# Sixty-four-column products of a recurrence, each given as two products of half the output partitions

## The chip, the cores and the metric

The kernel runs on one core of a Trainium2 chip. TensorE multiplies a stationary operand (up to 128 rows of contraction by 128 columns, which become output partitions) with moving columns and writes to PSUM. VectorE (DVE in the profile), ScalarE (ACT) and GpSimd (POOL) work on what it leaves, and SyncE (SP) issues most DMAs. The metric is the device time of one execution in microseconds (us), lower is better. Before the change it is 2248.54 us, the median of three runs (2246.16 to 2250.44).

## The reference, cut to what matters

Two encoder layers over 256 tokens of width 1024: dilated attention and a dense SwiGLU, then bidirectional RWKV-7 time mixing and eight SwiGLU experts of which each token takes two. All is float32. The change is in the RWKV-7 recurrence, which the reference writes as a scan over tokens with one 64 x 64 state per head:

```python
def step(state, inp):
    r_t, w_t, k_t, v_t, a_t, b_t = inp
    sa = jnp.einsum('bhvk,bhk->bhv', state, a_t)
    state = state * w_t[:, :, None, :] + sa[..., None] * b_t[:, :, None, :] + v_t[..., None] * k_t[:, :, None, :]
    return state, jnp.einsum('bhvk,bhk->bhv', state, r_t)
...
y_f = wkv_scan(rf, decay[0], k_dir[0], vf, -kk, kk * a[0], reverse=False)
y_b = wkv_scan(rf, decay[1], k_dir[1], vf, -kk, kk * a[1], reverse=True)
```

There are 16 heads of 64 features and two directions.

## The kernel before, in words

The kernel has no scan over tokens. Time is cut in two chunks of 128 tokens (t = 0, 1), and inside a chunk the recurrence is a triangular system of 128 x 128 for each head and direction. Heads are handled in four quarters (q = 0 to 3) of four heads. A set is one of the four pairs of direction and chunk.

For each quarter TensorE makes, in the order of its one queue:

- `decay_sums`, `cumulated`, `ends`: sums over time from which ScalarE takes exponentials, and from these VectorE the scaled keys (L1814 to L1835);
- `operands` (transposes, L920 and L921) and `system`: products over 64 rows, two heads side by side on the lower and the upper 64 rows of the array;
- `pairings`: again 64 rows, two heads side by side, evicted by VectorE with a mask (L1863, L1865, L1866);
- `values`: for each of four heads a product of a 128 x 128 stationary matrix with the 64 columns of that head's values (`z0`, PSUM bank 7), evicted by ScalarE (L1455), and a second such product that `add_y` (L957) accumulates in bank 4;
- `head_turn`: the solve. The early chunk of both directions goes first (steps z1 to z5, width 64), the late chunk after it with the width 128. The helper `four` gives the four products of a step, and VectorE (L1897, L1904) or ScalarE (L1474) evicts them before the next step of the same direction may start (`need`). The two directions alternate, so that one's products cover the other's eviction. Products that were already 64 output partitions wide are z5 and the chunk states (`St`).

The turns are software pipelined. `head_turn(q)` also gives the decay sums, operands and systems of quarter q + 1, and it ends with `all_pairings(q + 1)`; VectorE meanwhile computes that quarter's keys among the z evictions, and in the late half the inverse of 16 x 16 diagonal blocks by many small linked instructions (L1876, L1878), which go out and come back by DMA (`td`, `gt_in`). A turn takes some 68 us, and all four with the first pairings run from 726.6 to 986 us.

`run` (L682) gives one chain of accumulating products to one output; `mm` is the plain matmul. A float32 product leaves two MATMUL records and two LDWEIGHTS records in the trace, called two passes below; a transpose leaves one. In the shapes of the profile, `128*128 128x64` is a pass with 128 contraction rows, 128 stationary columns and 64 moving columns, and `128*64` one with 64 stationary columns, `64*128` one with 64 contraction rows.

Of the kernel before, what the change touches and what calls it, by code (L numbers as in the profile page):

```python
# [22 lines left out]
P = 128  # L23
# [16 lines left out]
RH = 64  # L40
RQ = 256
# [101 lines left out]
def build(nc, x_in, pos_in, const_in, mask_in, vec_in, rows_in, qk_rows, qk_cols, wqkv, awo, wrkv, w0, w1, w2, a0, a1, a2,  # L143
          g1, g2, bwo, fw13, fw2, router, mw13, mw2, out):
    ctx = ExitStack()
    with ctx:
        arena = ctx.enter_context(nc.sbuf_tensor("arena", [P, 53200], F32))
        ps = ctx.enter_context(nc.psum_tensor("ps", [P, 8, 512], F32))
# [152 lines left out]
        for d in range(2):  # L301
            o = {}
# [20 lines left out]
        gm23 = [[lent.take(4, P) for _ in range(2)] for _ in range(2)]  # L323
# [58 lines left out]
        def at_set(q, i):  # L382

            return q * 4 + i + 1
# [291 lines left out]
        def _(pe):  # L676
            mm = pe.matmul

            def run(o, pairs, **kw):

                for n, (a, b) in enumerate(pairs):
                    last = mm(o, a, b, start=(n == 0), stop=(n == len(pairs) - 1))  # L682
                return last

            def rms_transposes(n, src, t, bank0):

                pe.wait_ge(rms_xn, n * T + t + 1)
                for b in range(4):
                    for f in range(2):
                        c = (2 * b + f) * P  # L690
                        last = pe.transpose(ps[:, bank0 + b, f * S + t * P:f * S + (t + 1) * P], src[:, t, c:c + P], ident)  # L691
                    last.then_inc(rms_tp, 1)
# [74 lines left out]

            pe.wait_ge(in_const, 16)
            rms_transposes(0, attn, 0, 0)
            rms_transposes(0, attn, 1, 0)  # L770
            for hg in range(HG):
                def qk_transposes(j):
# [11 lines left out]
                for j in range(18):  # L784
                    u = hg * 9 + j // 2
                    c = hg * 18 + j
                    t = j % 2
# [5 lines left out]
                    for k in range(KB):  # L793
                        if c == 0:
                            pe.wait_ge(rms_h, k + 1)
                        last = mm(ps[:, 4 + c % 2, :], hT[:, k, t * P:(t + 1) * P], w[:, k, :], start=(k == 0), stop=(k == KB - 1))  # L796
# [20 lines left out]
                for j in range(8):  # L817
                    h, t, c = j // 2, j % 2, hg * 8 + j
# [3 lines left out]
                    for b in range(4):  # L822
                        last = pe.transpose(ps[:, 6, b * P:(b + 1) * P], probs[:, c % 3, b * P:(b + 1) * P], ident)
# [4 lines left out]
                    if c >= 2:  # L828
# [3 lines left out]
                                           (pT[:, c % 2, 2], v[:, t, 1, hc]), (pT[:, c % 2, 3], v[:, t, 2, hc])]).then_inc(o_ps, 1)  # L832
            back_transposes(attn, 0, oT_ps, (o_sb, 16))
            out_projection(0, U_QKV, oT, (oT_sb, 4), lambda: rms_transposes(1, attn, 0, 4))

            rms_transposes(1, attn, 1, 4)
# [6 lines left out]
            for half in range(2):  # L843
                for n in range(2):
                    w = unit(RKV0 + n).rearrange("p (k n) -> p k n", n=512)
                    for t in range(T):
                        for k in range(4 * half, 4 * half + 4):
                            if (n, t) == (0, 0):
                                pe.wait_ge(mix_ready, k + 1)
                            last = mm(ps[:, 4 + 2 * n + t, :], MIXES[0][2][:, k, t * P:(t + 1) * P], w[:, k, :], start=(k == 0), stop=(k == KB - 1))  # L850
# [24 lines left out]
            def value(q, t, h):  # L875
                return rkv[:, 2, t, q * RQ + h * RH:q * RQ + (h + 1) * RH]
# [76 lines left out]

            def add_y(t, h, lhsT, rhs, first=False, last=False):

                c = t * RQ + h * RH
                return mm(ps[:, 4, c:c + RH], lhsT, rhs, start=first, stop=last, skip_group_check=True)  # L957

            def values(q, i):

                d, t = SETS[i]
                if i == 0 and q:
                    pe.wait_ge(Y.sb, q)
                pe.wait_ge(gm.sb, q * 8 + 2 * i + 2)
                if i:
                    pe.wait_ge(z0.sb, at_set(q, i - 1))
                for h in range(4):
                    c = h * RH
                    last = run(ps[:, 7, c:c + RH], [(gm23[i % 2][0][:, h, :], value(q, t, h))])
                last.then_inc(z0.ps, 1)  # L970
                for h in range(4):
                    add_y(t, h, gm23[i % 2][1][:, h, :], value(q, t, h), first=(i == 0 and h == 0))

            def all_pairings(q):

                pe.wait_ge(X.sb, 4 * (q + 1))
                pairings(q, 0)
                pairings(q, 1)
                values(q, 0)
                pairings(q, 2)  # L980
                values(q, 1)
                pairings(q, 3)
                values(q, 2)
                values(q, 3)

            def chain_of(q, late):


                turn = [16 * late]

                def four(done, of, by, width=P, rows=slice(0, P)):

                    bank = 5 + turn[0] % 3
                    turn[0] += 1
                    for h in range(4):
                        last = run(ps[rows, bank, h * width:(h + 1) * width], [(of[:, h, rows], by[:, h, :])])
                    last.then_inc(done.ps, 1)

                return four, turn
# [5 lines left out]
            def head_turn(q):  # L1005
# [51 lines left out]
                def early_y():  # L1057

                    for d in range(2):
                        need(z5, 0, d)  # L1060
                        for h in range(4):
                            add_y(d, h, gm1[2 * d][:, h, :], ze[d][0][:, h, :])
# [70 lines left out]
                for d in range(2):  # L1133
                    for h in range(4):
                        add_y(1 - d, h, gm1[2 * d + 1][:, h, :], zl[d][0][:, h, 0:RH])
# [56 lines left out]
            for t in range(T):  # L1192
                for n in range(2):
                    if (t, n) == (1, 1):
                        rms_transposes(3, xn, 0, 0)
                    for k in range(4, KB):
                        last = mm(ps[:, 4 + 2 * n + t, :], moT[:, k, t * P:(t + 1) * P], w[n][:, k, :], start=False, stop=(k == KB - 1))  # L1197
# [5 lines left out]
            for t in range(T):  # L1203
                last = run(ps[:, 4, t * EXPERTS:(t + 1) * EXPERTS], [(hT[:, k, t * P:(t + 1) * P], rw[:, k, :]) for k in range(KB)])
# [89 lines left out]
            with pe.Fori(0, EXPERTS // 2 - 1) as i:  # L1294
                for e in range(2):
                    n = i * 2 + e
                    one_expert(n, e, i, (lambda: row_transposes(n + 2, 0), lambda: row_transposes(n + 2, 1)))
            n = EXPERTS - 2
# [6 lines left out]
            with pe.Fori(0, OVER) as j:  # L1305
                with pe.If(j < many):
# [3 lines left out]
                    n = j + EXPERTS  # L1310
# [1069 lines left out]
```

## Time and profile before

| | |
|---|---|
| median of the three runs | 2248.54 us |
| the profiled execution's own time | 2250.66 us |
| its span, first to last instruction | 2248.8 us |
| mean granted TensorE clock | 0.988 |
| TensorE busy | 2178.3 us, 97% |
| VectorE busy | 429.4 us, 19% |
| chain that ended last | PE 92%, DVE 4%, ACT 2%, DMA 1%, issue 1% |

A PE record begins when the pass begins, and its end is modelled, so that passes overlap in the records; the distance between starts is the pace. A row of a group gives the count of records, the time in which at least one of them ran, the mean length of one in ns and the idle time before them with what ended it. Idle times under 0.15 us are not named.

### The profile page before, as it was taken

To read this page: it belongs to the slowest core of one execution; us is meant where nothing else is said; L and a number is where in the kernel's file an instruction comes from. 1 tells how busy PE (TensorE), PEld (TensorE's weight loads), DVE (VectorE), ACT (ScalarE), POOL (GpSimd) and SP (SyncE) were. 2 spreads that over 40 slices of the span, in tenths; PEclk is the share of its full clock that TensorE was granted. 3 is DMA by queue.
4 is the path that set the end of the run, shared out by engine and by line. 5 is a ranking of instruction groups with operands and counts; after the bars stand their busy time and mean duration, and the time that the engine had idled before them with its cause. 6 is when DMAs were issued, how large, how long until landed. Compare 5 with 4: busy or idle time off the path is not lost.

```text
span 2248.8 us, 19811 instructions
## 1 busy us (share of the span) xinstructions
PE 2178.3 (97%) x7756; PEld 1209.4 (54%) x7756; DVE 429.4 (19%) x960; ACT 296.0 (13%) x661; POOL 196.8 (9%) x318
## 2 busy tenths in 40 slices
PE   8999989999899999997999999999999999999998
PEld 3454456776455999875444444444444444444443
DVE  2131231000445467434000000000000000000100
ACT  2121130000012543310000000000000000000000
POOL 1111101000104354200000000000000000000000
PEclk9999999999999999997999999999999999999999
DMA  9433425445410110236988989889898898999991
GB/s 346 150 113 112 150 75 187 150 150 164 150 33 9 19 26 16 79 101 222 323 300 302 308 287 322 300 301 308 299 308 300 296 314 298 307 308 299 340 301 60
DMA packets 353293, 474.12 MB, mean 211 GB/s; under 512 B 30104, under 2 KB 288432, under 8 KB 353216
## 3 DMA queue, kind: packets, MB, share of 16 engines
q1 hardware_dynamic: 349856, 460.96, 61.3%
q0 software_dynamic: 2336, 8.42, 1.1%
q10 hardware_dynamic: 1024, 3.67, 0.4%
q8 instruction: 52, 0.85, 0.2%
q14 instruction: 25, 0.20, 0.0%
HBM read 460.96 MB, written 12.06 MB: 210 GB/s over the span
## 4 chain that ended last, share of the span: by engine, by line
PE 92%; DVE 4%; ACT 2%; DMA 1%; issue 1%; POOL 0%; SPq 0%; DVEq 0%; POOLq 0%
PE ps L682 47%; PE ps L1283 17%; PE ps L796 11%; PE ps L734 7%; PE ps L747 2%; PE ps L957 1%; PE ps L850 1%; PE ps L1258 1%; PE ps L763 1%; PE ps L1190 1%; PE ps L1197 0%; PE ps L781 0%; DMA arena<-yd,arena 0%; ACT arena L1439 0%; PE ps L691 0%
## 5 line engine op out<-in xcount | busy, mean ns | idle before, releaser
L682 PE MATMUL ps<-arena 128*128 128x512 f32 (+10 forms) x4290 | 1160.9, 435 | 28.4 <-ACT arena L1381 6.8
L682 PEld LDWEIGHTS ps<-arena 128*128 128x128 f32 (+3 forms) x4290 | 628.0, 188 | 509.8 <-issue 460.7
L1283 PE MATMUL ps<-arena 128*128 128x512 f32 x896 | 394.4, 593 | 1.5 <-ACT arena L1567 0.6
L1283 PEld LDWEIGHTS ps<-arena 128*128 128x128 f32 x896 | 165.8, 190 | 190.7 <-issue 190.7
L796 PE MATMUL ps<-arena 128*128 128x512 f32 x576 | 253.3, 596 | 2.6 <-DVE arena L1633 2.6
L2093 DVE TENSOR_TENSOR arena<-arena,ps 128x256 f32<-128x256 f32 x112 | 47.2, 421 | 999.7 <-ACT arena L1574 998.7
L796 PEld LDWEIGHTS ps<-arena 128*128 128x128 f32 x576 | 108.0, 191 | 129.3 <-issue 126.0
L1574 ACT ACTIVATE arena<-ps 128x256 f32<-128x256 f32 x112 | 43.1, 385 | 999.3 <-PE ps L682 999.3
L734 PE MATMUL ps<-arena 128*128 128x256 f32 x704 | 153.9, 381 | 0.0
L734 PEld LDWEIGHTS ps<-arena 128*128 128x128 f32 x704 | 134.6, 191 | 20.2 <-issue 1.9
L2343 POOL DMA_INDIRECT arena<-yd,arena x4 | 3.8, 957 | 1040.7 <-DMA yd<-arena 1039.8
L1258 PEld LDWEIGHTS ps<-arena 128*128 128x128 f32 x224 | 31.3, 141 | 55.3 <-issue 54.3
L747 PE MATMUL ps<-arena 128*128 128x512 f32 x128 | 55.6, 592 | 0.0
L1474 ACT ACTIVATE arena<-ps 128x512 f32<-128x512 f32 (+1 forms) x80 | 44.2, 559 | 54.7 <-PE ps L682 54.7
L1567 ACT ACTIVATE arena<-ps 128x256 f32<-128x256 f32 x112 | 42.4, 379 | 49.8 <-PE ps L1258 49.8
L1672 DVE TENSOR_TENSOR arena<-arena,ps 128x256 f32<-128x256 f32 x22 | 9.3, 422 | 198.6 <-ACT arena L1338 198.6
L1258 PE MATMUL ps<-arena 128*128 128x128 f32 x224 | 42.8, 273 | 0.2 <-DVE arena L2093 0.2
L1718 DVE TENSOR_REDUCE arena<-arena 128x4 f32<-128x512 f32 x24 | 16.5, 686 | 131.0 <-ACT arena L1363 131.0
L957 PE MATMUL ps<-arena 128*128 128x64 f32 x320 | 40.3, 277 | 0.0
L747 PEld LDWEIGHTS ps<-arena 128*128 128x128 f32 x128 | 24.3, 190 | 28.9 <-issue 28.7
L957 PEld LDWEIGHTS ps<-arena 128*128 128x128 f32 x320 | 37.8, 192 | 1.3 <-issue 0.7
L2257 POOL TENSOR_TENSOR arena<-arena 128x256 f32<-128x256 f32 (+4 forms) x70 | 34.7, 496 | 5.5
(238 smaller groups left out, 968.7 us busy)
## 6 DMA issues: line engine op xcount, KB each, us to landing
arena<-mw SPq DMA_DIRECT2D x336, 1024.0 KB, 6.9
arena<-wqkv SPq DMA_DIRECT2D x36, 1024.0 KB, 7.5
arena<-fw SPq DMA_DIRECT2D x32, 1024.0 KB, 6.9
arena<-wrkv SPq DMA_DIRECT2D x12, 1024.0 KB, 7.4
arena<-awo SPq DMA_DIRECT2D x4, 1024.0 KB, 6.3
xg<-arena POOLq DMA_DIRECT2D x8, 512.0 KB, 10.0
arena<-bwo SPq DMA_DIRECT2D x4, 1024.0 KB, 8.6
arena<-xg SPq DMA_DIRECT2D x7, 512.0 KB, 7.7
```

Source lines behind the costliest of these rows:

```text
L682: last = mm(o, a, b, start=(n == 0), stop=(n == len(pairs) - 1))
L734: last = mm(ps[:, c % 4, side * S:(side + 1) * S], w[:, k, side * S + f * P:side * S + (f + 1) * P], src[:, k, :], start=(k == 0), stop=(k ...
L747: last = mm(ps[:, 4 + 2 * t + h, :], hid[:, n % 2, k, t * P:(t + 1) * P], w[:, k, h * 512:(h + 1) * 512], start=(n == 0 and k == 0), stop= ...
L796: last = mm(ps[:, 4 + c % 2, :], hT[:, k, t * P:(t + 1) * P], w[:, k, :], start=(k == 0), stop=(k == KB - 1))
L957: return mm(ps[:, 4, c:c + RH], lhsT, rhs, start=first, stop=last, skip_group_check=True)
L1258: last = pe.transpose(ps[:, 3, at:at + P], hid_e[:, g % 2, f * P:(f + 1) * P], ident)
L1283: last = mm(ps[:, 5 + h, :], hidT[:, g % 2, k, :], w[:, k, h * 512:(h + 1) * 512], start=(g == 0 and k == 0), stop=(g == GE // 2 - 1 and k ...
L1474: act.activation(dst.rearrange("p a b -> p (a b)"), ps[:, bank, 0:4 * width], ACT.Copy).then_inc(s.sb, 1)
L1567: act.activation(hidT[:, g // 2 % 2, g % 2 * 2:g % 2 * 2 + 2, :].rearrange("p a b -> p (a b)"), ps[:, 3, g % 2 * 256:g % 2 * 256 + 256], A ...
L1574: act.activation(sg_e[:, g % 2, :], ps[:, g % 3, 0:256], ACT.Silu).then_inc(sge_sb, 1)
L2093: dve.tensor_tensor(hid_e[:, g % 2, :], sg_e[:, g % 2, :], ps[:, g % 3, 256:512], ALU.mult).then_inc(hide_sb, 1)
L2257: link(pool.tensor_tensor(v[:, :, :, 0:width], v[:, :, :, 0:width], v[:, :, :, width:2 * width], ALU.add))
```

## The change

A product with 64 moving columns and 128 stationary columns is given as two, each with 64 of the stationary columns, one for output partitions 0 to 63 and one for 64 to 127. Both read the same moving columns. It is done in `add_y`, in the `z0` products of `values`, and in `four` where the width is 64 and all partitions are written (z1 to z4 of the early chunk). No wait and no signal moves; the signal stays on the last product of each group.

```diff
+            COLS = (slice(0, RH), slice(RH, P))
+
+            def by_halves(o, pairs):
+
+                for n, (a, b) in enumerate(pairs):
+                    for c in COLS:
+                        last = mm(o[c], a[:, c], b, start=(n == 0), stop=(n == len(pairs) - 1))
+                return last
...
             def add_y(t, h, lhsT, rhs, first=False, last=False):
 
-                c = t * RQ + h * RH
-                return mm(ps[:, 4, c:c + RH], lhsT, rhs, start=first, stop=last, skip_group_check=True)
+                at = t * RQ + h * RH
+                for c in COLS:
+                    ins = mm(ps[c, 4, at:at + RH], lhsT[:, c], rhs, start=first, stop=last, skip_group_check=True)
+                return ins
...
-                    last = run(ps[:, 7, c:c + RH], [(gm23[i % 2][0][:, h, :], value(q, t, h))])
+                    last = by_halves(ps[:, 7, c:c + RH], [(gm23[i % 2][0][:, h, :], value(q, t, h))])
...
                     for h in range(4):
-                        last = run(ps[rows, bank, h * width:(h + 1) * width], [(of[:, h, rows], by[:, h, :])])
+                        o = ps[rows, bank, h * width:(h + 1) * width]
+                        product = by_halves if width == RH and rows == slice(0, P) else run
+                        last = product(o, [(of[:, h, rows], by[:, h, :])])
```

## Rows read from the trace of the kernel before

**Rows 1.** The page, part 1: busy us (share of the span), instructions.

```profile
PE 2178.3 (97%) x7756; PEld 1209.4 (54%) x7756; DVE 429.4 (19%) x960; ACT 296.0 (13%) x661; POOL 196.8 (9%) x318
```

**Rows 2.** Three stages by windows: engines' busy us (instructions), PEclk, DMA share, GB/s.

```profile
core 0: us, PE busy (x) PEld busy (x) DVE busy (x) ACT busy (x) POOL busy (x), PEclk, DMA share, GB/s
...
726.60:986.00 259.40, 252.31 (x2260) 233.82 (x2260) 145.55 (x289) 100.27 (x199) 91.57 (x121) 0.99 0.13 33
986.00:2248.80 1262.80, 1239.26 (x3148) 568.62 (x3148) 100.50 (x255) 88.51 (x245) 11.58 (x12) 0.99 0.86 289
```

**Rows 3.** Groups by shape, whole run, TensorE products with 64 moving columns.

```profile
L682 PE MATMUL ps<-arena 128*128 128x64 f32 x384 | 47.5, 276 | 0.0
...
L957 PE MATMUL ps<-arena 128*128 128x64 f32 x320 | 40.3, 277 | 0.0
```

**Rows 4.** The same view of the weight loads.

```profile
L957 PEld LDWEIGHTS ps<-arena 128*128 128x128 f32 x320 | 37.8, 192 | 1.3 <-issue 0.7 <-DVE arena L1904 0.2
```

**Rows 5.** Groups by shape, window 777.03 to 778.00: state products, halves in turn.

```profile
L682 PE MATMUL ps<-arena 128*64 128x64 f32 x31 | 1.1, 226 | 0.0
```

**Rows 6.** Groups by shape, window 761.44 to 762.43: z5, one half after the other.

```profile
L682 PE MATMUL ps<-arena 128*64 128x64 f32 x15 | 1.2, 228 | 0.0
```

**Rows 7.** Timeline of TensorE around 762: start us, us, instruction, [idle before].

```profile
759.78 2.88 PE L682 MATMUL ps<-arena 128*128 128x64 f32 x30
762.59 0.33 PE L920 MATMUL ps<-arena 128*128 128x128 f32 x1
762.76 0.27 PE L921 MATMUL ps<-arena 128*128 128x128 f32 x1
762.87 0.27 PE L920 MATMUL ps<-arena 128*128 128x128 f32 x1
```

**Rows 8.** Timeline, turn 0's end: the next quarter's pairings.

```profile
794.11 0.69 DVE L1961 COPY arena<-ps 128x512 f32<-128x512 f32 x1
...
805.02 0.68 DVE L1866 TENSOR_TENSOR arena<-ps,arena 128x512 f32<-128x512 f32 x1
...
806.12 1.06 PE L682 MATMUL ps<-arena 128*128 128x64 f32 x8
...
807.01 1.06 PE L957 MATMUL ps<-arena 128*128 128x64 f32 x8
...
807.90 21.34 PE L682 MATMUL ps<-arena 65*128 65x256 f32 x156
...
811.10 1.68 DVE L1814 SCALAR_TENSOR_TENSOR arena<-arena 128x512 f32<-128x512 f32 x1 [5.40 <-ACT arena L1417]
```

**Rows 9.** Timeline, turn 1's head: key scaling on VectorE among the z steps.

```profile
818.84 0.74 DVE L1828 SCALAR_TENSOR_TENSOR arena<-arena 128x512 f32<-128x512 f32 x1 [2.28 <-ACT arena L1425]
...
824.02 0.42 DVE L1897 TENSOR_TENSOR arena<-ps,arena 128x256 f32<-128x256 f32 x1 [0.43 <-PE ps L682]
...
826.67 0.42 DVE L1897 TENSOR_TENSOR arena<-ps,arena 128x256 f32<-128x256 f32 x1 [0.18 <-PE ps L682]
...
828.38 0.39 ACT L1474 ACTIVATE arena<-ps 128x256 f32<-128x256 f32 x1 [2.29 <-PE ps L682]
```

**Rows 10.** Timeline of VectorE, turn 1's late half.

```profile
845.99 1.25 DVE L1942 TENSOR_TENSOR arena<-ps,arena 64x128 f32<-64x128 f32 x4 [5.36 <-PE ps L682]
848.94 0.69 DVE L1897 TENSOR_TENSOR arena<-ps,arena 128x512 f32<-128x512 f32 x1 [1.70 <-PE ps L682]
...
861.49 0.33 DVE L1878 TENSOR_REDUCE arena<-arena 128x13 f32<-128x169 f32 x1
```

**Rows 11.** Timeline of TensorE around 945.7, the last turn's start.

```profile
945.69 12.56 PE L682 MATMUL ps<-arena 128*128 128x128 f32 x96 [2.16 <-DMA arena<-td]
```

**Rows 12.** Timeline of VectorE at the recurrence's end.

```profile
985.30 0.69 DVE L1961 COPY arena<-ps 128x512 f32<-128x512 f32 x1 [2.95 <-PE ps L957]
```

**Rows 13.** Windows around that start: same columns as Rows 2.

```profile
946.00:951.50 5.50, 5.50 (x38) 5.50 (x36) 0.00 (x0) 2.10 (x4) 1.60 (x2) 0.69 1.02 387
```

## The prediction, made before the changed kernel was run

> **What bounds the kernel now.** I read first the page's busy shares: TensorE 97% of the span, VectorE 19% [rows 1]. Then the stages. The change touches only 726.6 to 986 us; behind it lie 1262.8 us of dense layers in which TensorE is again 98% busy (1239.26 us) and DMA 0.86 [rows 2]. That tail will start earlier by what the recurrence gives; it won't shrink. Within the 259.4 us TensorE shows 252.31 us busy, but VectorE 145.55, over half of it, and its queue is a chain with small linked operations. So the third view had to be the timeline of both engines, place by place: a pass saved on TensorE is worth something only where VectorE isn't the one that keeps it waiting.
>
> **What one product costs, and what two halves cost.** The touched products are 384 + 320 = 704 passes, 352 products [rows 3]. In a steady stretch eight such passes start 0.89 us apart from the next eight (806.12, 807.01, 807.90) [rows 8]: 111.5 ns a pass. The mean record of 276 ns is latency, not pace. The moving side is only half as wide as in a 128-column product, so it isn't the moving columns that set 111.5 ns but the load of 128 stationary columns: 320 loads take 37.8 us together, 118 ns each with the pauses between [rows 4].
>
> The halves are not in this trace, but two near rows bound them. The state products have halves in turn: 31 records begin in 0.97 us [rows 5], 31 ns apiece with a longer first step, so two halves of a pass start in about 60 ns. In z5, eight passes in a row go to the same half: 15 records in 0.99 us with one longer step between the directions [rows 6], so some 60 ns each, and two of them one after the other take 120. The new code alternates the halves, two passes to each. The state products alternate as well, in fours, so I take the row of the state products: 60 ns for two halves. The difference that stays open is that here both halves read the same moving columns, there each its own. So the saving is 51.5 ns a pass, 0.41 us for a block of four products (8 passes), and 704 x 51.5 = 36.3 us on TensorE if nothing else moves. The other end is 704 x (111.5 - 120) = 6.0 us lost.
>
> **What the change of shape costs.** From 64-column passes back to full ones the steps are 0.15 and 0.17 us (the last z5 pass begins at about 762.43, one record of 0.228 [rows 6] before the end of its row, 762.66; then 762.59, 762.76) where they are 0.11 after [rows 7]: against the 0.06 and 0.11 of a steady stream, 0.14 us too much. The entry is hidden in rows of one line, and I take it as the exit, 0.14 (between 0 and 0.3). New pairs of switches are needed round z1 and round z2, as full-width products stand between: 0.56 a turn. Before the decay sums one exit is added, 0.14, and round `early_y` about 0.17. z3 and z4 now join z5 without a switch, and `add_y` joins the preceding 64-column `Rq` products. In all about 0.7 us a turn.
>
> **Where the saving arrives.** I go through the recurrence in order.
>
> (A) First pairings, 729.7 to 740.2: 8 blocks, 8 x 0.41 = 3.3. The last `z0` block needs VectorE's third masked eviction; in the same place a turn later that ends at 805.70 and TensorE comes at 806.12 [rows 8]: 0.42 of cover against two shortened blocks, 0.82. So 0.45 comes back as a wait, and 0.14 for the exit: 2.7.
>
> (B) Head of turn 0, z1 to z4: 8 blocks, 3.3, less 0.56 for switches, less waits. An eviction answers 0.78 us after a block's last pass begins (record 0.28 [rows 3], ACT 0.39 [rows 9], 0.11 for signals, an estimate), and the other direction's block now covers only 0.5. So some 0.3 each before z4 and z5 and z3, 0.9 in all: 1.85.
>
> (C) `early_y`, 2 blocks, 0.82 less 0.17: 0.65 in turns 0 to 2. In the last turn it waits for z5's eviction: 0.35.
>
> (D) The late half of turns 0 to 2. Up to the state products VectorE sits idle for TensorE (5.36 and 1.70 us before 845.99 and 848.94), and from there its linked operations and evictions run without a named pause to the copy of y [rows 10]. The 4 blocks of `add_y` in it (1.65 us) therefore buy nothing: worth 0.
>
> (E) Pairings at the end of turns 0 and 1. VectorE works from 794.11 to 805.70, copy, masks, inverse, copies [rows 8]. TensorE's first blocks only wait longer. Behind 805.70 TensorE now needs 2.2 us to the decay sums at 807.90, and after the change 2 blocks of 0.48 and 0.08 for signal and exit: 1.15 saved, and it arrives, as VectorE is then 5.40 us idle until those sums have passed [rows 8]. Twice 1.15. At the end of turn 2 the next turn waits for the inverse's DMA, 2.16 us already [rows 11], fed by VectorE: only 0.2.
>
> (F) Heads of turns 1 and 2. VectorE scales keys from 818.84 and makes z2 and z3 in between, with 0.43 and 0.18 us of idle for TensorE [rows 9]. Those 0.6 us can go, then z3's eviction at 826.67 sets z4, and z4's two blocks (0.8) are on the path again: 1.4 each. The head of turn 3 has no next keys: as (B), 1.85.
>
> (H) End of turn 3: no inverse is left, VectorE is idle 2.95 us for `add_y` before its copy at 985.30 [rows 12], and 4 blocks arrive in full: 1.65.
>
> Sum: 2.7 + 1.85 + 3 x 0.65 + 0.35 + 2 x 1.15 + 0.2 + 2 x 1.4 + 1.85 + 1.65 = 15.65 us of the 36.3 - 2.6 that TensorE saves. Half the saving is lost to VectorE. Nothing stands late behind 986 us but the chain of norm, router and weights, which moves along: the ring of weights is refilled when the last pairings are through, and it moves with them.
>
> The profiled execution took 2250.66 us, 2.1 above the median, so it would take 2235.0; from the median 2248.54 the forecast is 2232.9.
>
> **Rivals.** *First, the halves don't run side by side* (same contraction rows, same moving columns). Mechanism and place: in every touched block the second half starts only when the first has been loaded and passed, at z5's pace. Then a pass costs 120 against 111.5, 6.0 us over 704, and the switches 2.6 more: slower, up to 8.6; where VectorE leads, a part is hidden, say 6: 2254.5. It decides from 111 ns a pair upwards. For it: no row has two halves with common moving columns. Against it: the state products [rows 5]. The Trainium skill speaks for it: its page "TensorE: Matmul & The Clock Gate", section "The mechanism" of the part on packing, says that a weight load overlaps products in flight only when the row group differs, and two column halves have the same rows. By that rule the second half could not overtake, and the time would be this rival's or above. In the trace the state products don't obey it.
>
> *Second, VectorE gives less room and the clock drops.* After (E) TensorE waits about 2 us in one piece. After 2.16 us of idle at 945.69 the granted clock is 0.69 in the next 5.5 us, half speed for a good 3 us [rows 11, 13]. Three to six new waits of this size, each up to 1.7 us where TensorE leads, take back some 4 to 8 us: 2240. For it: that row; against it: most of those waits lie where VectorE sets the pace, and the slowness would be covered.
>
> *Third, the saving arrives in full*, because VectorE's order has slack that 0.15-us idle times hide: 33.7 us off, 2215. Against it: the unbroken rows of (D) and (E).
>
> *Fourth, nothing moves* (0, 2248.5): VectorE's chain is the only bound. Against it: its 5.4 us of idle twice a turn [rows 8, 10].
>
> **How the numbers follow.** Forecast 0.64, its own range 2227 to 2239 (pairs at 56 to 70 ns, waits a third more or less). Slower rival 0.13, second 0.14, third 0.05, fourth 0.04. The range of 2223 to 2245 leaves out the first, third and fourth, 0.22 less their near edges, so about 0.2. About 4.5 us (0.2%) can be told from no change. Faster by more: 0.62 + 0.13 + 0.05 = 0.80; within: 0.02 + 0.01 + 0.04 + 0.02 of the slower rival = 0.09; slower 0.11.
>
> **What would show it.** Right: 128*64 128x64 records 192 + 1408 = 1600 and none of 128*128 128x64, starts some 30 ns apart; the stage 726.6 to 986 shorter by 15 to 16 and the tail as long as before; new idle of TensorE before the third pairings (VectorE L1863) of near 2 us, and before the last `add_y` of turns 0 to 2 (L1955); the late half of turns 0 to 2 as long as before. Wrong: a pair that takes over 100 ns, a tail that changes its length, a late half that shrinks by more than 0.5 us a turn, or a turn that keeps its 68 us.

## The result, and the profile after

The changed kernel takes 2232.14 us (median of six runs, 2229.74 to 2239.85), the kernel before, run beside it, 2250.14 (six runs, 2246.16 to 2252.57): a ratio of 0.9929, 95% interval 0.9908 to 0.995. Between the medians that is 18.0 us less, by the ratio 16.0 (11 to 21). In two later sessions the unaltered new kernel stood at 0.9913 (0.99 to 0.9927) and 0.9899 (0.9885 to 0.9914), with medians 20.6 and 21.8 us below those of the kernel before. The forecast was 15.65 us less. That its 2232.9 us lies within 0.8 of the median is partly luck: the saving is larger than forecast (19.2 us in the recurrence, below), and the kernel before measured 1.6 us higher this time.

Part 1 of the page after, against [rows 1]. There are 704 more TensorE instructions, one more per halved pass.

```profile
PE 2147.7 (96%) x8460; PEld 1172.7 (52%) x8460; DVE 434.1 (19%) x960; ACT 295.2 (13%) x661; POOL 198.8 (9%) x318
```

The two later stages by windows, columns as in [rows 2], first of the profiled run after:

```profile
core 0: us, PE busy (x) PEld busy (x) DVE busy (x) ACT busy (x) POOL busy (x), PEclk, DMA share, GB/s
...
726.90:967.07 240.17, 221.45 (x2964) 197.80 (x2964) 150.31 (x289) 99.78 (x198) 93.76 (x121) 0.99 0.14 36
967.07:2237.90 1270.83, 1239.12 (x3148) 568.13 (x3148) 100.42 (x255) 88.37 (x245) 11.56 (x12) 0.99 0.86 288
```

and of a second profiled run of the same kernel (the first experiment):

```profile
726.70:966.88 240.18, 221.45 (x2965) 197.79 (x2965) 150.44 (x289) 99.76 (x198) 93.78 (x121) 0.99 0.13 36
966.88:2228.70 1261.82, 1238.80 (x3148) 568.15 (x3148) 100.51 (x255) 88.38 (x245) 11.55 (x12) 0.99 0.86 290
```

The recurrence took 259.4 us [rows 2] and takes 240.2 in both. TensorE's busy time there fell by 30.9 us (252.31 to 221.45), the stage by 19.2: the remaining 11.6 us are new idle time. The tail is as long as before in the second run (1261.82 against 1262.80) and 9.0 us longer in the first, although TensorE is busy equally long. Of these, 1.0 us is a wait in the middle of the tail (at 1326.62, on nothing that the profile shows), and 7.6 us lie behind TensorE's last product, which begins 18.9 us before the end in the first run and 11.3 in the second. There TensorE's queue jumps three times over the body of the loop for overflowing experts. The one line's view on TensorE's sequencer (count, shortest/median/longest ns, first and last start), first run, then second:

```profile
L1319 PEldq COMPARE_BRANCH  x3: 232/3912/9014, 2222.9 to 2237.2; - x3
```

```profile
L1319 PEldq COMPARE_BRANCH  x3: 221/221/4326, 2221.5 to 2227.1; - x3
```

In order of time the three jumps take 3.9, 9.0 and 0.2 us in the first run and 4.3, 0.2 and 0.2 in the second, so it is the second jump that is longer, by 8.8 us. The kernel before has 3.7, 0.2 and 0.2. So the first profiled run, 2239.85 us, is no example of the tail.

The groups by shape in the recurrence, after, against [rows 3]. All 704 whole passes with 64 moving columns are gone, and 768 + 640 = 1408 halves have come.

```profile
L691 PE MATMUL ps<-arena 128*64 128x64 f32 x768 | 29.8, 228 | 1.8 <-DVE arena L1879 1.0 <-DVE arena L1910 0.5
L967 PE MATMUL ps<-arena 128*64 128x64 f32 x640 | 23.8, 223 | 2.7 <-DVE arena L1968 2.6
L682 PE MATMUL ps<-arena 64*128 64x128 f32 x224 | 20.3, 299 | 11.4 <-DVE arena L1876 9.1 <-ACT arena L1452 1.6 <-ACT arena L1410 0.7
...
L682 PE MATMUL ps<-arena 128*64 128x64 f32 x192 | 9.4, 227 | 0.1
```

The same row before:

```profile
L682 PE MATMUL ps<-arena 64*128 64x128 f32 x224 | 20.0, 296 | 3.4 <-ACT arena L1439 1.6 <-DVE arena L1863 1.1 <-ACT arena L1397 0.7
```

Most of the saving stops in that row: its idle time grew from 3.4 to 11.4 us, and the growth is in pairings that wait for VectorE's masked evictions (L1876 to L1879, before L1863 to L1866), 9.1 us against 1.1. The rest is in front of `add_y` (L967, 2.7 us, none before) and of z0 and z1 to z4 (L691, 1.8 us, none before). TensorE's timeline at turn 0's end, against [rows 8]:

```profile
786.81 1.15 PE L967 MATMUL ps<-arena 128*64 128x64 f32 x32 [0.87 <-DVE arena L1968]
787.89 1.58 PE L682 MATMUL ps<-arena 64*128 64x128 f32 x16
790.34 1.58 PE L682 MATMUL ps<-arena 64*128 64x128 f32 x16 [0.87 <-DVE arena L1876]
791.85 0.69 PE L691 MATMUL ps<-arena 128*64 128x64 f32 x16
792.36 0.64 PE L967 MATMUL ps<-arena 128*64 128x64 f32 x16
792.93 1.58 PE L682 MATMUL ps<-arena 64*128 64x128 f32 x16
...
797.78 1.58 PE L682 MATMUL ps<-arena 64*128 64x128 f32 x16 [2.19 <-DVE arena L1876]
799.30 0.69 PE L691 MATMUL ps<-arena 128*64 128x64 f32 x16
799.81 0.64 PE L967 MATMUL ps<-arena 128*64 128x64 f32 x16
800.77 0.69 PE L691 MATMUL ps<-arena 128*64 128x64 f32 x16 [0.33 <-DVE arena L1879]
801.29 0.64 PE L967 MATMUL ps<-arena 128*64 128x64 f32 x16
801.86 5.39 PE L682 MATMUL ps<-arena 65*128 65x256 f32 x31
```

A block of eight pairs (x16) begins 0.51 us before the next (791.85, 792.36), where eight whole passes took 0.89. Within the block the records begin 7 and 51 ns apart by turns: 58 ns a pair. Only the switch of shape behind it makes the next step 0.57 (792.36 to 792.93). The waits stand where the prediction put them: 2.19 us before the third pairings, 0.87 before the last `add_y`.

At the recurrence's end VectorE waited 2.95 us for the last `add_y` [rows 12], now 1.25:

```profile
966.32 0.69 DVE L1974 COPY arena<-ps 128x512 f32<-128x512 f32 x1 [1.25 <-PE ps L967]
```

Place by place, as differences between starts of the same instructions in the profiled runs (recurrence, in us):

| place of the prediction | before | forecast | after minus before |
|---|---|---|---|
| A first pairings to decay sums | 13.52 | -2.7 | -2.77 |
| B decay sums to operand transposes, turn 0 | 22.42 | -1.85 | -1.94 |
| C on to the late half, turns 0 to 2 | 8.88 | -0.65 each | -0.70 each |
| D late half to copy of y, turns 0 to 2 | 22.64 | 0 | 0.02, -0.01, 0.01 |
| E copy of y to decay sums, turns 0, 1 | 13.79 | -1.15 each | -0.93, -0.92 |
| F as B, turns 1 and 2 | 22.42 | -1.4 each | -1.91 each |
| copy of y in turn 2 to start of turn 3 | 16.11 | -0.2 | -0.75 |
| turn 3 to its copy of y | 39.61 | -3.85 | -6.03 |
| sum | | -15.65 | -19.24 |

### The profile page after: what moved, and what is told of

Same layout as the page of the kernel before. It is cut to its first block, busy times and chain, and to the rows that moved or that the text cites. A ratio compares the mean times of both kernels' runs of the same rounds, so it can differ in the third digit from the quotient of the medians.

```text
span 2237.9 us, 21219 instructions
## 1 busy us (share of the span) xinstructions
PE 2147.7 (96%) x8460; PEld 1172.7 (52%) x8460; DVE 434.1 (19%) x960; ACT 295.2 (13%) x661; POOL 198.8 (9%) x318
## 4 chain that ended last, share of the span: by engine, by line
PE 89%; DVE 5%; ACT 2%; DMA 1%; issue 1%; SPq 0%; POOL 0%; DVEq 0%; POOLq 0%
PE ps L682 44%; PE ps L1296 17%; PE ps L805 11%; PE ps L743 7%; PE ps L756 2%; PE ps L859 1%; PE ps L1271 1%; PE ps L772 1%; PE ps L1203 1%; DVE arena L1889 1%; PE ps L691 1%; PE ps L1210 0%; PE ps L790 0%; DMA arena<-wqkv 0%; DMA arena<-yd,arena 0%
## 5 line engine op out<-in xcount | busy, mean ns | idle before, releaser
L682 PE MATMUL ps<-arena 128*128 128x512 f32 (+9 forms) x3906 | 1117.6, 450 | 36.5 <-DVE arena L1876 9.1
L682 PEld LDWEIGHTS ps<-arena 128*128 128x128 f32 (+2 forms) x3906 | 582.0, 187 | 515.7 <-issue 459.5
L1296 PEld LDWEIGHTS ps<-arena 128*128 128x128 f32 x896 | 165.8, 190 | 190.7 <-issue 190.7
L805 PEld LDWEIGHTS ps<-arena 128*128 128x128 f32 x576 | 108.0, 191 | 129.2 <-issue 126.2
L1587 ACT ACTIVATE arena<-ps 128x256 f32<-128x256 f32 x112 | 42.9, 383 | 1000.3 <-PE ps L682 1000.3
L743 PEld LDWEIGHTS ps<-arena 128*128 128x128 f32 x704 | 134.9, 192 | 20.4 <-issue 1.9
L1271 PEld LDWEIGHTS ps<-arena 128*128 128x128 f32 x224 | 31.3, 141 | 55.2 <-issue 54.3
L1580 ACT ACTIVATE arena<-ps 128x256 f32<-128x256 f32 x112 | 42.4, 378 | 49.7 <-PE ps L1271 49.6
L756 PEld LDWEIGHTS ps<-arena 128*128 128x128 f32 x128 | 24.3, 190 | 28.9 <-issue 28.7
L1351 ACT ACTIVATE arena<-ps 128x256 f32<-128x256 f32 x22 | 8.4, 383 | 202.1 <-PE ps L743 202.1
L1376 ACT ACTIVATE arena<-ps 128x512 f32<-128x512 f32 x24 | 14.3, 597 | 155.5 <-PE ps L805 155.5
## 6 DMA issues: line engine op xcount, KB each, us to landing
xg<-arena POOLq DMA_DIRECT2D x8, 512.0 KB, 10.2
```

The lines of the kernel that those rows point to most:

```text
L743: last = mm(ps[:, c % 4, side * S:(side + 1) * S], w[:, k, side * S + f * P:side * S + (f + 1) * P], src[:, k, :], start=(k == 0), stop=(k ...
L756: last = mm(ps[:, 4 + 2 * t + h, :], hid[:, n % 2, k, t * P:(t + 1) * P], w[:, k, h * 512:(h + 1) * 512], start=(n == 0 and k == 0), stop= ...
L1271: last = pe.transpose(ps[:, 3, at:at + P], hid_e[:, g % 2, f * P:(f + 1) * P], ident)
L1296: last = mm(ps[:, 5 + h, :], hidT[:, g % 2, k, :], w[:, k, h * 512:(h + 1) * 512], start=(g == 0 and k == 0), stop=(g == GE // 2 - 1 and k ...
L1580: act.activation(hidT[:, g // 2 % 2, g % 2 * 2:g % 2 * 2 + 2, :].rearrange("p a b -> p (a b)"), ps[:, 3, g % 2 * 256:g % 2 * 256 + 256], A ...
L1587: act.activation(sg_e[:, g % 2, :], ps[:, g % 3, 0:256], ACT.Silu).then_inc(sge_sb, 1)
```

## The experiments

**The new kernel once more**, and the same with one guard round the overflow loop. The theory of these two: the 9.0 us jump is what spreads the runs.

> The changed kernel, unaltered, once more. Its profiled execution took 2239.85 us while four of its six executions took 2229.7 to 2233.1, and in the profile the last jump of TensorE's queue over the body of the overflow loop lasts 9.0 us (2227.6 to 2236.6). Theory: the recurrence is always 19 us shorter, and this jump costs some executions 7 us more at the very end. Expect a median of 2230 to 2233, single executions either near 2230 or near 2239, none between. Rival: the 9 us were a disturbance of that one execution; then all executions lie within 3 us of 2230.

> The changed kernel with one condition around TensorE's overflow loop, so that its queue jumps once over the loop when no token overflows, in place of three times over its body. Nothing computed changes. Theory (the jump costs): executions near 2239 vanish or become rarer, since SyncE's output transfer (5 us) covers one jump of 4 us; median 2228.5 to 2231. Rival (something else delays the end): the same two groups of times as the unaltered kernel.

```diff
-            with pe.Fori(0, OVER) as j:
-                with pe.If(j < many):
+            with pe.If(many > 0):
+                with pe.Fori(0, OVER) as j:
+                    with pe.If(j < many):
...
```

The body of the loop stays as it is. Unaltered: 2230.48 us (2229.69 to 2235.14). One of the five runs, 2235.14, lies between the two groups that the theory named, and 4.7 us above the median, so neither expectation held. Guarded: 2231.42 (2228.39 to 2236.65), ratio 0.9919 (0.9905 to 0.9932) against 0.9913 (0.99 to 0.9927). The guard changes neither median nor spread, so these jumps aren't shown to spread the runs. A jump of 9.0 us was seen in one profile; what makes it long, and what spreads the other runs, is open.

**Order of the halves.** Four lower halves of a block first, then four upper ones, in `four`, z0 and `add_y` alike:

> The changed kernel with the same halves in another order: in every block of four products all four lower halves first, then all four upper halves, so that neighbours in the queue go to the same half of the array. Theory (the gain comes from two halves running side by side): like z5 each pass takes 58 to 60 ns, two in sequence 117 to 120 against 111.5 before, a block takes 0.94 to 0.96 us against 0.42 to 0.46 in turns; the time is 2250 to 2256, as slow as before or slower. Rival (the gain comes from the shorter loads alone, the order is free): 2230 to 2233 as the changed kernel. Third possibility: the queue looks ahead over eight passes and overlaps the end of the lower halves with the start of the upper, giving 2240 to 2250.

```diff
...
-                for h in range(4):
-                    add_y(t, h, gm23[i % 2][1][:, h, :], value(q, t, h), first=(i == 0 and h == 0))
+                for half in COLS:
+                    for h in range(4):
+                        add_y(t, h, gm23[i % 2][1][:, h, :], value(q, t, h), first=(i == 0 and h == 0), cols=(half,))
...
```

2242.78 us (2239.6 to 2249.8, ten runs), ratio 0.9966 (0.9956 to 0.9977), recurrence 250.41: about half of the gain is gone. The theory's time (2250 to 2256) was too long, and the third possibility (2240 to 2250) came true. Of the 10.2 us lost in the recurrence some 1.6 are the clock: turn 3 begins behind 2.04 us of idle, and the granted clock is 0.69 in the 5.5 us that follow (what such a stretch costs comes below). TensorE's timeline where z0 (here L682) passes into `add_y` (L967):

```profile
729.38 0.27 PE L967 MATMUL ps<-arena 128*64 128x64 f32 x1
729.44 0.22 PE L682 MATMUL ps<-arena 128*64 128x64 f32 x1
729.49 0.22 PE L967 MATMUL ps<-arena 128*64 128x64 f32 x1
729.50 0.22 PE L682 MATMUL ps<-arena 128*64 128x64 f32 x1
729.55 0.22 PE L967 MATMUL ps<-arena 128*64 128x64 f32 x1
729.55 0.22 PE L682 MATMUL ps<-arena 128*64 128x64 f32 x1
729.61 0.74 PE L967 MATMUL ps<-arena 128*64 128x64 f32 x13
730.28 1.90 PE L682 MATMUL ps<-arena 64*128 64x128 f32 x19
```

Each group of halves goes at 58 ns a pass, and only about three or four passes of the other half run beside it, where one group meets the next: here the last upper passes of z0 between the first lower ones of `add_y`, and likewise where lower and upper passes of one block meet. The two blocks take 1.47 us (728.81 to 730.28), against 1.08 by turns and 1.78 whole. So a half alone costs 58 ns, a pair by turns costs 58 ns too, and the gain is running side by side, not loading less: two halves in sequence cost 116, more than the whole pass with 111.5. The first rival needed a pair to cost 120 with the halves by turns; the 58 ns refute it. It leaned on a rule of the Trainium skill, "TensorE: Matmul & The Clock Gate", section "The mechanism" of the part on packing, that a weight load overlaps products in flight only when the row group differs. The trace doesn't agree for these halves: they share all 128 rows, and a pair costs the 58 ns of one.

**One part alone: `add_y`.**

> Only the products of add_y are given in halves (320 of the 704 passes); z0 and the steps z1 to z4 are whole as before. Theory: those of the late half of turns 0 to 2 (128 passes with the last turn's 32) buy nothing in three turns, as VectorE leads there. What is left: first pairings 4 blocks less more switches (z0 and add_y alternate, 0.28 a set), about 0.5 to 1; early_y 0.65 in three turns and 0.35; the last turn's 4 blocks 1.65; later pairings 0.3 each. Sum 4.5 to 5.5 us, so 2245 against 2250. Rival (every saved pass counts): 320 x 51.5 ns less 20 switches, 13 us, so 2237.

```diff
-                        product = by_halves if width == RH and rows == slice(0, P) else run
+                        product = run
```

and z0 by `run` as well. 2246.47 us (2243.4 to 2254.4, ten runs), ratio 0.9985 (0.9974 to 0.9996); recurrence 254.04, 5.35 less than before, as expected.

**The other part alone: z1 to z4.**

> Only the products of the linked steps (z1 to z4) are halved; the pairings' z0 and add_y are whole again, as before. My theory (the parts add up; add_y alone gave 5.35 us of the 19.2): the recurrence is 19.2 - 5.3 less what the z0 blocks bring of themselves (2 to 3 us), so 11 to 12 us shorter than before, time near 2239; heads of turns 0 to 2 shorter by 1.9 each, as in the whole change, late halves of turns 0 to 2 the same length (22.64). It also tests the 2.2 us by which the last turn gave more than forecast. If they come from the half-clock stretch (3.4 us at half speed that before lies at 946.3, behind 2.16 us of idle, in the head of turn 3, and after lies at 926.4, where VectorE leads): here that stretch either stays in turn 3's head, and the head then gives only about 2.0, or it is gone from there, and it gives 3.7. Rival: the clock has nothing to do with it, and the head of turn 3 gives 3.7 with a half-clock stretch in it. Second rival (parts don't add up since VectorE's room is shared): under 9 us in all.

2241.04 us (2240.08 to 2242.86), ratio 0.9957 (0.9943 to 0.9971); recurrence 248.88, 10.51 less than before, just under the 11 to 12 expected. The heads of turns 0 to 2 give 1.99 each, and the last turn gives 3.63 with no half-clock stretch in its head. Its start, against [rows 11], and its clock, against [rows 13]:

```profile
938.86 3.39 PE L682 MATMUL ps<-arena 128*128 128x128 f32 x28 [1.24 <-DMA arena<-td]
```

```profile
938.86:944.40 5.54, 5.54 (x70) 5.35 (x71) 0.00 (x0) 3.15 (x6) 2.74 (x3) 1.00 0.96 368
```

With `add_y` alone the idle time there was 2.56 us, the half clock followed (0.69 in the next 5.5 us), and the turn gave 2.34. What a half-clock stretch costs in this place is told by the next runs.

**VectorE's linked chain taken out, from both kernels.**

> The kernel before without the small linked multiplications and reductions of VectorE by which the inverses of quarters 1 to 3 are formed (the old values are used again; this part of the computation is left out). It takes about 9 us of VectorE's chain out of each of turns 0 to 2. Together with the same edit of the kernel after it tells what keeps the saving from arriving. Here TensorE already leads nearly everywhere: late halves go from 22.64 to about 22.2 (the length of the late half of turn 3, which has no inverse), pairings give 0.5 a turn, the DMA wait before turn 3 (2.16 us) shrinks: 3 to 5 us in all, 2246 to 2248.

> The kernel after without the same multiplications and reductions of quarters 1 to 3. My theory (VectorE's linked chain holds back the saving of add_y and of the pairings): late halves of turns 0 to 2 fall from 22.64 to about 20.6 (the late half of turn 3), pairings from 12.86 to about 10.5; the recurrence is 27 to 30 us shorter than that of the kernel before with the same edit, against 19.2 with the inverses in; time 2217 to 2220. Rival (the rest is lost on TensorE itself, in changes of shape and slower pairs than 58 ns): the difference of the two stays at 19 to 20 us, time near 2227.

```diff
-                for i in range(lo, hi):
+                for i in range(lo, hi if q == 0 else lo):
```

Both edited kernels leave out that part of the computation. Before, so edited: 2247.42 us (2244.26 to 2249.1), recurrence 253.83, 5.6 shorter where 3 to 5 were expected. After, so edited: 2226.66 (2222.28 to 2229.77), recurrence 232.27. The difference is 21.6 us in the recurrence; my number was 27 to 30, the rival's 19 to 20, and the time is the rival's (near 2227). In the places it speaks clearly for VectorE, and in the sum it doesn't:

| place | before, whole / without | after, whole / without |
|---|---|---|
| late half, turns 0 to 2 | 22.64 / 22.30 | 22.65 / 20.61 |
| copy of y to decay sums | 13.79 / 13.43 | 12.86 / 10.78 |
| head of turns 1, 2 | 22.42 / 22.42 | 20.51 / 21.73 |
| turn 3 to its copy of y | 39.61 / 37.98 | 33.58 / 35.09 |

In the first two rows the change saves 1.69 and 2.65 us a turn once the chain is gone, against 0 and 0.93 with it: there VectorE did hold the saving back. But then the next bounds appear. TensorE's timeline in turn 1's head and at turn 3's start, after without the chain:

```profile
803.09 5.57 PE L682 MATMUL ps<-arena 128*128 128x128 f32 x40 [0.62 <-DMA arena<-td]
...
818.23 1.15 PE L691 MATMUL ps<-arena 128*64 128x64 f32 x32 [0.49 <-DVE arena L1910]
```

```profile
924.38 3.80 PE L682 MATMUL ps<-arena 128*128 128x128 f32 x18 [2.99 <-DMA arena<-td]
```

The inverse's way through DMA and VectorE's key scaling take 1.2 us a turn back, and turn 3 starts with 2.99 us of idle and a half-clock stretch. The window from that start:

```profile
924.38:929.90 5.52, 5.52 (x39) 5.40 (x41) 0.00 (x0) 1.91 (x4) 4.03 (x4) 0.71 1.00 374
```

The edited kernel before, in turn, waits only 0.33 us there and keeps its clock:

```profile
939.79 5.46 PE L682 MATMUL ps<-arena 128*128 128x128 f32 x47 [0.33 <-DMA arena<-td]
```

```profile
939.79:945.30 5.51, 5.51 (x49) 5.51 (x50) 0.00 (x0) 2.77 (x5) 3.95 (x4) 1.00 0.99 367
```

Turn 3 has no inverse to leave out, so its 37.98 against 39.61 us is the price of the half-clock stretch in the whole kernel before: 1.63 us. The kernels after give nearly the same, 35.09 with a stretch against 33.58 without: 1.51. Since of the two edited kernels only the one after has it, the difference of 21.6 would be some 23 us without, an estimate from these two numbers, still short of 27.

**Three tries to give VectorE room**, and the new kernel beside two of them.

> The kernel after, with the copy of y (0.69 us) and the two copies of the finished inverse (0.63 and 0.71 us) of turns 0 to 2, and the last copy of y, moved from VectorE to ScalarE, which is idle there for 10.2, 2.2 and 4.5 us. All lie in the stretch in which TensorE waits for VectorE's masked evictions (0.87 and 2.19 us of idle before pairings). My theory: each turn's pairings end up to 2.0 us earlier, three times, and what follows goes with them: 5 to 6 us shorter than the kernel after, near 2225. Rival one: the evictions of z0 on ScalarE are held up by its new copies, and the inverse comes through DMA no earlier, so that turn 3 gains nothing: 3 to 4 us. Rival two: TensorE's own work sets those stretches after all: under 1 us.

> The kernel after, unaltered, so that the three others of this group stand beside it on the same chip. 2230 to 2232 us, recurrence 240.2 us. The two theories of the next runs (VectorE's chain against TensorE's own work as the bound of the pairings) say the same of it.

> The kernel after with only the copy of y (0.69 us on VectorE) moved to ScalarE. Moving the inverse's copies as well brought 1.35 us a turn twice, but the DMA that carries the inverse came no earlier and turn 3 lost it again (3.67 us of idle and a half-clock stretch in turn 3's head, which costs 1.6 us). Here the inverse's copies stay on VectorE and come 0.6 us earlier with the rest. My theory: 0.6 us in each of three turns, 1.8 us in the recurrence; with the wait for the inverse's DMA before turn 3 near 1.1 us, as in the kernel after, and no half-clock stretch in turn 3's head. Rival: the copy is late on ScalarE, frees the bank late, and add_y's bank is what the next pairings wait for: 0 or slower.

> As the run with the copy of y on ScalarE, and before turn 3 VectorE finishes the inverse first (rows 14 and 15 and its two copies, 3.8 us) and then does all four sets of masked evictions. VectorE's sum stays the same. My theory: the last masked eviction ends when it did, the inverse is in place by then, and the 1.06 us of waiting for its DMA before turn 3 go: 2.8 us less than the kernel after in the recurrence, near 2228. Rival: with four sets in one piece VectorE waits for TensorE's products of the third set, since these need banks that the first evictions free: the 1.06 us are only moved, 1.8 us in all, or less.

```diff
+                act.wait_ge(Y.ps, q + 1)
+                act.wait_ge(head_done, q + 1)
+                act.activation(y_sum.rearrange("p t n -> p (t n)"), ps[:, 4, :], ACT.Copy).then_inc(Y.sb, 1)
...
-                dve.tensor_copy(y_sum.rearrange("p t n -> p (t n)"), ps[:, 4, :]).then_inc(Y.sb, 1)
```

| kernel | us (range) | ratio (interval) | recurrence |
|---|---|---|---|
| new, beside the next two | 2230.29 (2228.37 to 2233.97) | 0.9899 (0.9885 to 0.9914) | 241.80 |
| copy of y moved | 2229.79 (2227.45 to 2231.32) | 0.9897 (0.9882 to 0.9911) | 238.82 |
| and inverse first in turn 2 | 2232.11 (2227.24 to 2237.92) | 0.9909 (0.9895 to 0.9923) | 239.71 |
| y and inverse copies moved | 2230.69 (2228.44 to 2231.83) | 0.9913 (0.9897 to 0.993) | 238.47 |

The last row is from another session than the first three. None can be told from the new kernel. In the traces each shortens the recurrence of 240.2 us by 0.5 to 1.7, all less than expected. With all copies moved, turns 1 and 2 are 1.3 and 1.2 us shorter (the third pairings begin at 795.02, 857.89 and 920.90, 62.9 and 63.0 us apart, not 64.2), and turn 3 gives a part back, since the DMA with the inverse is no earlier, and half clock follows (0.72 in the next 5.5 us):

```profile
928.71 5.28 PE L683 MATMUL ps<-arena 128*128 128x128 f32 x32 [3.67 <-DMA arena<-td]
```

With the inverse first, that wait did go, but VectorE's four sets in one piece left TensorE 3.12 us idle before the third pairings. With the copy of y alone one turn is 63.41 us long (between the starts of its decay sums), 0.8 less than 64.2, as expected and a little more, but the next is 64.42: behind its wait of 2.03 us the granted clock is 0.69 in the 5.5 us from 858.20.

The repeated run of the unaltered kernel shows a chance element. Its second waiting place at 863 fell into half clock; in the first repeat the same place did not. The window behind the same instruction in both, first the one with the lower clock:

```profile
862.97:868.50 5.53, 5.34 (x81) 4.31 (x82) 3.12 (x5) 0.84 (x3) 4.89 (x8) 0.71 0.26 45
```

```profile
861.80:867.30 5.50, 5.18 (x87) 4.44 (x88) 2.88 (x5) 2.05 (x3) 4.92 (x8) 1.00 0.26 45
```

Both times the idle time before was 2.19 or 2.20 us. It made that recurrence 1.6 us longer (241.80 against 240.18). In the first repeat the third such place has the lower clock instead, 0.69 behind 2.19 us of idle at 925.97, and there it costs nothing: the start of turn 3 waits for DMA anyway, and comes 15.4 us after the copy of y in both. In the second repeat that wait for DMA is 2.44 us long, longer than before the change, and full clock follows it:

```profile
935.39 1.83 PE L682 MATMUL ps<-arena 128*128 128x128 f32 x14 [2.44 <-DMA arena<-td]
```

```profile
935.39:940.89 5.50, 5.50 (x69) 5.31 (x70) 0.00 (x0) 3.15 (x6) 2.69 (x3) 1.00 0.99 372
```

**Halves for products with 128 moving columns too.**

> The kernel after with the products of 128 moving columns in the linked steps (ET, E, E2T and the late z1 to z4, 640 passes) also given as two halves of 64 stationary columns. Two theories of why a pair of halves takes 58 ns where a whole pass took 111.5. Theory one: the load of 128 stationary columns sets 111.5, and side by side only the moving columns count, 64 of them 58 ns, so 128 of them about twice that: the Rq products, whose halves alternate with 128 moving columns each, take 109 ns a pair. Then these passes go from 111.5 to 109: 1.6 us on TensorE, and the changes of shape go too (0.14 us each, about four a turn in the heads): 1 to 3 us less than the kernel after. Theory two: halves run side by side cost 58 ns whatever moves, or are held up by the doubled number of instructions: then 640 passes give 34 us on TensorE and well over 10 us in the time, or, the other way, the time is longer.

```diff
-                        product = by_halves if width == RH and rows == slice(0, P) else run
+                        product = by_halves if rows == slice(0, P) else run
```

2236.3 us (2229.05 to 2243.83), ratio 0.9924 (0.9907 to 0.9942), recurrence 243.6: nothing gained, and rather slower than the new kernel beside it (0.9899, 0.9885 to 0.9914), though the intervals overlap. TensorE's timeline, late ET and E in turn 0:

```profile
768.34 5.46 PE L691 MATMUL ps<-arena 128*64 128x128 f32 x96
773.63 1.15 PE L682 MATMUL ps<-arena 128*64 128x64 f32 x32
```

The 48 pairs take 5.29 us to the next line, 109 or 110 ns each; whole passes take 111.5. So a pair of halves costs what its moving columns cost: 58 ns for 64, 109 for 128. Theory one holds in the price of a pair; its gain of 1 to 3 us did not appear. In this run turn 3 waited 3.35 us for DMA with 6.8 us of half clock around it, where the unaltered kernels wait 1.06 to 2.44; whether the doubled instructions cause that wasn't separated from chance. Up to the copy of y of turn 2 the recurrence is 0.8 us shorter than that of the repeat beside it (191.3 against 192.1), which also has one stretch of half clock before.

## Why the prediction was right, and where its sizes were off

*The price of a pair* (60 ns): measured 58, 0.51 us a block. (The 118 ns a load beside it were misread: busy time holds no pauses [rows 4], but the records of neighbouring loads overlap. The pace of 111.5 stands on [rows 8].) Taking the alternating state products as the model was the step that mattered, and the serial order shows why: what counts is that neighbours in the queue go to different halves. The difference left open, common moving columns here and separate ones there, made none.

*VectorE keeps half the saving* (D and E): right. D stays at 22.64, and without the linked chain it falls by 2.0 us. In the sum less is shown: without the chain the change saves 21.6 us and not 19.2, because the next bounds follow close. E was forecast at 1.15 and gave 0.93: behind VectorE's last eviction TensorE needs 1.14 us to the decay sums (800.72 to 801.86), 1.06 less than before, and VectorE's own stretch from the copy of y became 0.14 longer (11.73 against 11.59), which the forecast had held constant.

*Heads of turns 1 and 2* (F, 1.4): mis-sized, 1.91 measured. Here I misread the kernel: I charged the key scaling only from turn 1 on [rows 9], but turn 0 prepares a next quarter as well. VectorE's timeline of the kernel before shows the same line in turn 0's head, 67.73 us before 818.84:

```profile
751.11 1.10 DVE L1828 SCALAR_TENSOR_TENSOR arena<-arena 128x512 f32<-128x512 f32 x1 [3.27 <-ACT arena L1425]
```

So B and F had to have one number, and B's 1.85 was the better one. In the new kernel the key scaling costs nothing there; it holds TensorE back only when everything before it is faster (0.49 us without the chain).

*Turn 3's start* (0.2): 0.75. TensorE waits for DMA before and after, and the inverse came 0.74 us sooner after the copy of y. Why, no run tells; with z1 to z4 alone it was 0.91, with `add_y` alone -0.14.

*The last turn* (1.85 + 0.35 + 1.65 = 3.85): 6.03, the largest miss. Three parts. `add_y` alone gives 2.34, where 2.0 was forecast: `early_y` doesn't lose half its gain to z5's eviction. The z steps give 2.0 for 1.85 (3.63 less 1.63). And 1.63 is the clock: the half-clock stretch that stood in turn 3's head before [rows 13] is not there in any of the three profiles of the new kernel, and all three turns take 33.57 or 33.58 us. The shorter wait alone doesn't explain it. In the first two the idle time before turn 3 is 1.08 and 1.06 us instead of 2.16 [rows 11], but partly because the half clock came one wait earlier, at the third pairings; in the third it is 2.44, and the clock stays full, with the stretch two waits earlier. With z1 to z4 alone the wait is 1.24, no new wait stands before it, and the clock stays full too. So neither the length of this wait nor a stretch taken over by a new wait explains it alone; why full clock follows there isn't shown. There is only one profile of the kernel before, and since the clock behind such a wait is partly chance, how often it pays these 1.63 us isn't known. I had used this row only for a rival, as a danger of new waits, and not asked whether the old stretch would stay. The sum of these parts is 2.34 + 2.0 + 1.63 = 5.97.

*The second rival* (clock lost behind new waits): its mechanism exists, its price mostly doesn't arrive. Of three new waits of 2.19 us one was followed by half clock in each profile of the new kernel. In the first two it was the last one, at the end of turn 2, and its cost fell into the wait for DMA that follows; in the third it was the one before, and cost 1.6 us. The rival's 4 to 8 us were seen in none. The third rival (saving in full) is refuted by D and E, the fourth (nothing) by A.

## What to carry to other kernels

Where a pass is bound by loading 128 stationary columns for few moving ones, split it into two column halves and issue them by turns: here 64 moving columns went from 111.5 to 58 ns, while four of one half first gave back half of it, and 128 moving columns gained only 2 ns. Count such a saving only up to the next engine in the chain, and expect a second bound (here DMA of the inverse and key scaling) right behind the first. When a change makes, moves or shortens waits of about 2 us, ask what clock follows each of them, and look at more than one profile.

## What the runs showed of the hardware that was not expected

Two halves with the same rows and the same moving columns run fully side by side (58 ns a pair). In serial order three or four passes of one group overlap with the other group, as if the engine found a partner only a few passes ahead; that reading was argued from one order, not tested with others. The clock after a wait of 2.2 us did not follow from its length: a granted clock of 0.71 behind one of two waits of 2.19 and 2.20 us, 1.00 behind the other, in runs of one kernel; and 1.00 behind 2.44 us, 0.69 behind 2.04, in two others. The second jump over the skipped loop at the end of TensorE's program took 0.2 us in one profile and 9.0 in another, and most of that difference (7.6 us) went into the time.
